# A transformer's third block on one Trainium2 core: router, token rows and routing in one stage, the table of rows by products of one-hot matrices, and LayerNorm in one stage

## What is computed

```python
hB = jax.nn.silu(layer_norm(hB, conv_ln_g, conv_ln_b))
yB = hB * jax.nn.silu(zB)
...
return layer_norm(r, ln_g, ln_b)
```

```python
logits = (h @ router_w + router_b).astype(jnp.float32)
top_v, top_i = lax.top_k(logits, TOP_K)
...
row_tok = jnp.full((n_blocks * MOE_BLOCK,), T, jnp.int32).at[dest].set(tok_sorted)
h_pad = jnp.concatenate([h, jnp.zeros((1, D), h.dtype)], axis=0)
xs = h_pad[row_tok].reshape(n_blocks, MOE_BLOCK, D)
```

## Time and profile before

| | |
|---|---|
| runs, us | 3936.74, 3937.1 (median), 3944.75 |
| profiled execution, us | 3943.41 |
| its span, us | 3941.2 |
| TensorE busy | 3407.6 us, 86% of the span |
| VectorE busy | 2309.9 us, 59% |
| ScalarE busy | 1537.9 us, 39% |
| GpSimd busy | 140.9 us, 4% |
| mean granted TensorE clock | 0.917 of full |

### The profile page before, as it was taken

How to read it: one execution, slowest core, us unless ns; L and a number is a source line. 1 busy time by engine, 2 the same in 40 slices (tenths; PEclk the granted TensorE clock), 3 DMA queues, 4 the chain that set the end, 5 groups by cost and what they waited for, 6 DMA issues and landing times. The chain is left out here.

```text
span 3941.2 us, 47465 instructions
## 1 busy us (share of the span) xinstructions
PE 3407.6 (86%) x16455; PEld 2632.6 (67%) x16456; DVE 2309.9 (59%) x2974; ACT 1537.9 (39%) x1920; POOL 140.9 (4%) x131
## 2 busy tenths in 40 slices
PE   7778898999968687899987977839999999999996
PEld 6546786874446467788764845637777777777774
DVE  4255765337322146455544384438888888888885
ACT  1154332010023341110113143217777777777772
POOL 0000000000000100000000000020000000000001
PEclk9879999999979888699997989959999999999997
DMA  5321222222111100022345201139999999999996
GB/s 168 92 70 33 85 96 84 97 86 86 65 32 48 33 17 1 17 93 98 105 152 205 96 1 41 47 140 411 363 352 351 355 361 351 358 356 359 355 348 227
DMA packets 189602, 653.68 MB, mean 166 GB/s; under 512 B 15081, under 2 KB 101193, under 8 KB 133042
## 3 DMA queue, kind: packets, MB, share of 16 engines
q1 hardware_dynamic: 171650, 605.44, 42.7%
q0 software_dynamic: 7568, 25.70, 1.7%
q10 hardware_dynamic: 10272, 21.02, 1.4%
HBM read 611.02 MB, written 36.77 MB: 164 GB/s over the span
## 5 line engine op out<-in xcount | busy, mean ns | idle before, releaser
L450 DVE TENSOR_TENSOR experts_rest<-experts_weights,experts_leading 128x2048 fp32r<-128x2048 f32 x384 | 875.1, 2286 | 100.0 <-ACT experts_leading L3122 100.0
L3122 ACT CAST experts_leading<-experts_weights 128x2048 fp32r<-128x2048 f32 x384 | 717.5, 1904 | 48.7 <-ACT experts_y L3114 24.3
L456 PE MATMUL psum<-experts_leading,experts_xT_leading 128*128 128x512 f32 x1024 | 411.7, 402 | 50.2 <-DVE experts_rest L450 50.2
L458 PE MATMUL psum<-experts_leading,experts_xT_rest 128*128 128x512 f32 x1024 | 410.7, 401 | 0.0
L457 PE MATMUL psum<-experts_rest,experts_xT_leading 128*128 128x512 f32 x1024 | 410.2, 401 | 0.0
L456 PEld LDWEIGHTS psum<-experts_leading,experts_xT_leading 128*128 128x128 f32 x1024 | 194.9, 190 | 109.1 <-DVE experts_rest L450 64.2
L457 PEld LDWEIGHTS psum<-experts_rest,experts_xT_leading 128*128 128x128 f32 x1024 | 195.9, 191 | 47.2
L458 PEld LDWEIGHTS psum<-experts_leading,experts_xT_rest 128*128 128x128 f32 x1024 | 195.8, 191 | 45.1
L456 PE MATMUL psum<-experts_leading,experts_hidden_leading 128*128 128x512 f32 x512 | 209.3, 409 | 0.0
L458 PE MATMUL psum<-experts_leading,experts_hidden_rest 128*128 128x512 f32 x512 | 203.0, 396 | 0.0
L457 PE MATMUL psum<-experts_rest,experts_hidden_leading 128*128 128x512 f32 x512 | 202.3, 395 | 0.0
(11 more groups left out here) (738 smaller groups left out, 6899.8 us busy)
## 6 DMA issues: line engine op xcount, KB each, us to landing
experts_weights<-in_w_up SPq DMA_DIRECT2D x256, 1024.0 KB, 6.8
experts_weights<-in_w_down SPq DMA_DIRECT2D x128, 1024.0 KB, 6.0
ada_unit<-in_w_ada SPq DMA_DIRECT2D x12, 2048.0 KB, 16.8
expert_rows<-experts_y ACTq DMA_DIRECT2D x66, 256.0 KB, 7.1
merge_first<-in_w_merge SPq DMA_DIRECT2D x16, 768.0 KB, 4.3
merge_weights<-in_w_merge SPq DMA_DIRECT2D x16, 768.0 KB
ff_up_first<-in_w_up SPq DMA_DIRECT2D x11, 1024.0 KB, 4.8
ff_up_weights<-in_w_up SPq DMA_DIRECT2D x11, 1024.0 KB
```

The source lines that it names most:

```text
L450: return dve.tensor_tensor(out, src, leading.bitcast(F32), ALU.subtract)
L456: pe.matmul(out, lh, rh, start=start, stop=False)
L458: return pe.matmul(out, ll, rh, start=False, stop=stop)
L3122: act.copy(leading[h % LEADING], place(ring, h)).then_inc(masked, 1)
```

## The change

- `feature_norm` can center: the chunks are summed in four stripes, ScalarE keeps the negative mean, TensorE spreads it to four banks, VectorE adds it to each chunk, and ScalarE alone squares. It can also apply another function than Identity with the shift, and multiply at the end. `feature_center`, and for branch B `activate` and `multiply`, are no longer called.
- The router's weights and bias and the experts' first bias are loaded in `moe_norm`.
- `route` takes in the tokens' rows and the router. The logits are formed with the weights as stationary operand, in four stripes that are then added by four small products. The rows' copies out of PSUM go to ScalarE.
- The 16 scatters, the fill, the load and the turn are gone. The table of rows is the sum of 16 products: (tokens' lane one-hot, 128 by 128) times (block one-hot weighted by token minus 512, 128 by 48).
- The first block's gather is issued at the end of `route`.

Diff, cut:

```diff
+def feature_norm(k, name, groups, scale, eps, shift=None, memory=(), then=None, center=False, func=ACT.Identity, times=None):
...
+                if center:
+                    act.wait_ge(added, 1)
+                    act.activation(mean[:, :], k.bank(2, P), ACT.Copy, scale=-1.0 / (len(flat) * P)).then_inc(averaged, 1)
...
+                    if center:
+                        act.wait_ge(centered, i + 1)
+                    if center or i % 2 == 0:
...
                         act.activation(sq[:, i % 4, 0:width[g]], s, ACT.Square).then_inc(squared[0], 1)
...
-                    act.activation(o, o, ACT.Identity, bias=shift[n]).then_inc(shifted, 1)
+                    act.activation(o, o, func, bias=shift[n]).then_inc(shifted, 1)
...
+                if center:
+                    for i, (_, _, s) in enumerate(flat):
+                        for j in range(STRIPES):
+                            last = pe.matmul(k.psum[j * STRIPE:(j + 1) * STRIPE, 2 * BANK:2 * BANK + P], k.c("ones")[:, 0:STRIPE],
+                                             s[:, j * P:(j + 1) * P], start=(i == 0), stop=(i == len(flat) - 1))
+                    last.then_inc(added, 1)
+                    pe.wait_ge(picked, 1)
+                    pe.wait_ge(averaged, 1)
+                    for j in range(STRIPES):
+                        rows = slice(j * STRIPE, (j + 1) * STRIPE)
+                        last = pe.matmul(k.bank(4 + j, P), first_rows[rows, :], mean[rows, :], start=True, stop=True)
+                    last.then_inc(placed, 1)
...
+                if center:
+                    dve.wait_ge(placed, 1)
+                    for _, _, s in flat:
+                        dve.tensor_tensor(striped(s), striped(s), striped(k.psum[:, 4 * BANK:8 * BANK])[:, :, 0:P], ALU.add
+                                          ).then_inc(centered, 1)
...
+                for n, (o, other) in enumerate(times or ()):
+                    dve.wait_ge(shifted, n + 1)
+                    dve.tensor_tensor(o, o, other, ALU.mult).then_inc(gated, 1)
...
-def feature_center(k, name, srcs):
...
-    feature_center(k, "ln2_center", chunks)
     feature_norm(k, "ln2", [(chunks, [k.x[:, n, :] for n in range(KD)], [k.p("ln_g", n) for n in range(KD)])],
-                 1.0 / D, "eps_2", shift=[k.p("ln_b", n) for n in range(KD)], then=ctx_load)
+                 1.0 / D, "eps_2", shift=[k.p("ln_b", n) for n in range(KD)], then=ctx_load, center=True)
...
-        feature_center(k, "conv_center", chunks)
         w_qc = first_unit(k, "proj2c", Section(d["w2_q_c"], 2, KD, None, None, None, chunks=2))
         feature_norm(k, "conv_ln", [(chunks, chunks, [k.p("conv_ln_g", n) for n in range(4)])], 1.0 / 512,
-                     "eps_2", then=w_qc.load)
-        activate(k, "conv_silu", ACT.Silu, [(acc[:, n, :], acc[:, n, :], k.p("conv_ln_b", n)) for n in range(4)])
-        multiply(k, "conv_gate", [(y[:, 4 + n, :], y[:, 4 + n, :], acc[:, n, :]) for n in range(4)])
+                     "eps_2", then=w_qc.load, shift=[k.p("conv_ln_b", n) for n in range(4)], center=True, func=ACT.Silu,
+                     times=[(y[:, 4 + n, :], acc[:, n, :]) for n in range(4)])
...
+    def load(self, k):
+        def then(sp, sem):
+            sp.dma_start(self.w[:, :], k.dram["router_w"][0, :, :]).then_inc(self.landed[0], 16)
+            sp.dma_start(self.bias[:, :], k.dram["router_b"][0:1, :].broadcast_to([P, EXPERTS])).then_inc(self.landed[0], 16)
+            sp.dma_start(self.b1[:, :], k.dram["b1_3"]).then_inc(self.landed[1], 16)
+        return then
...
+            @block.sync
...
+                sp.dma_start(residual, k.x[:, :, :].rearrange("p k t -> p (k t)")).then_inc(stored, 16)
+                sp.wait_ge(cleared, 1)
+                sp.dma_start(rows[T:T + 1, :], zero[:, :]).then_inc(rows_stored, 16)
+                for t in range(TT):
+                    sp.wait_ge(copied, 2 * t + 2)
+                    sp.dma_start(rows[t * P:(t + 1) * P, :], by_token[:, t, :]).then_inc(rows_stored, 16)
+                sp.wait_ge(rows_stored, 16 * (TT + 1))
+                sp.wait_ge(stored, 16 * 3)
+
+            @block.gpsimd
...
+                pool.memset(zero[:, :], 0.0).then_inc(cleared, 1)
+                pool.wait_ge(kept, 1)
+                pool.tensor_copy(index[:, 0:1], row_of[:, 0:1]).then_inc(indexed, 1)
+                pool.wait_ge(rows_stored, 16 * (TT + 1))
+                pool.wait_ge(indexed, 1)
+                pool.indirect_dma_start(out=x_rows[:, 0, :], out_offset=None, in_=rows,
+                                        in_offset=bass.IndirectOffsetOnAxis(ap=index[:, 0:1], axis=0)).then_inc(first_gathered, 16)
...
+                act.wait_ge(counted, 1)
+                act.copy(iota[:, :], k.bank(2, P)).then_inc(iota_kept, 1)
+                act.wait_ge(parted, 1)
+                act.copy(part_sums[:, :], k.bank(0)).then_inc(part_copied, 1)
+                act.wait_ge(b1_raised, 1)
+                act.activation(b1_leading[:, :], inputs.b1[:, :], ACT.Copy).then_inc(b1_masked, 1)
...
+                for n in range(2 * TT):
+                    act.wait_ge(turned, n + 1)
+                    act.copy(by_token[:, n // 2, (n % 2) * BANK:(n % 2 + 1) * BANK], k.bank(4 + n % 4)).then_inc(copied, 1)
...
+                act.wait_ge(blocked, 1)
+                for t in range(TT):
+                    mine = in_block[:, t, :, :].rearrange("p k b -> p (k b)")
+                    act.activation(mine, mine, ACT.Copy, scale=token[:, t:t + 1]).then_inc(weighted, 1)
...
+                pe.matmul(k.bank(2, P), k.c("ones"), k.c("before")[:, 0:P], start=True, stop=True).then_inc(counted, 1)
+                pe.wait_ge(inputs.landed[0], 32)
+                for kk in range(KD):
+                    j = kk % STRIPES
+                    last = pe.matmul(k.psum[j * STRIPE:(j + 1) * STRIPE, 0:T], inputs.w[:, kk * E:(kk + 1) * E], k.h[:, kk, :],
+                                     start=(kk < STRIPES), stop=(kk >= STRIPES))
+                last.then_inc(parted, 1)
+
...
+                turn(0)
+                pe.wait_ge(part_copied, 1)
+                for t in range(TT):
+                    last = pe.matmul(k.psum[:, BANK + t * E:BANK + (t + 1) * E], part_sums[:, t * P:(t + 1) * P], k.c("striped"),
+                                     start=True, stop=True)
+                last.then_inc(summed, 1)
+                for n in range(1, 2 * TT):
+                    turn(n)
...
+                pe.wait_ge(choice, TT)
...
+                last.then_inc(ranked, 1)
...
+                for t in range(TT):
+                    pe.wait_ge(weighted, t + 1)
+                    pe.wait_ge(laned, t + 1)
+                    for n in range(K):
+                        last = pe.matmul(k.psum[:, 6 * BANK:6 * BANK + B], in_lane[:, t, n, :], in_block[:, t, n, :],
+                                         start=(t == 0 and n == 0), stop=(t == TT - 1 and n == K - 1))
+                last.then_inc(placed, 1)
+                pe.wait_ge(passed_, 1)
...
+                pe.wait_ge(spreaded, TT)
+                for t in range(TT):
+                    last = pe.transpose(k.psum[0:E, 7 * BANK + t * P:7 * BANK + (t + 1) * P], spread[:, t, :], k.c("ident"))
+                last.then_inc(gated, 1)
...
+                dve.wait_ge(summed, 1)
+                v.do(dve.tensor_tensor(logits[:, :, :], k.psum[:, BANK:BANK + TT * E].rearrange("p (t e) -> p t e", e=E),
+                                       inputs.bias[:, :].unsqueeze(1).broadcast_to([P, TT, E]), ALU.add))
...
-                v.then(dve.tensor_copy(toks[:, :], k.c("lanes_on")))
-                v.then(dve.memset(fill[:, :], T))
...
+                v.do(dve.tensor_scalar(ratio[:, :, :], dest_f[:, :, :], 1.0 / P, None, ALU.mult))
+                dve.wait_ge(iota_kept, 1)
+                v.do(dve.tensor_tensor(edges[:, :, :, :].rearrange("p t k b -> p (t k) b"),
+                                       iota[:, 0:B + 1].unsqueeze(1).broadcast_to([P, TT * K, B + 1]),
+                                       ratio[:, :, :].rearrange("p t k -> p (t k)").unsqueeze(2).broadcast_to([P, TT * K, B + 1]),
+                                       ALU.is_le))
+                dve.tensor_tensor(in_block[:, :, :, :], edges[:, :, :, 0:B], edges[:, :, :, 1:B + 1], ALU.subtract).then_inc(blocked, 1)
+                v.do(dve.tensor_reduce(block_of[:, :, :], edges[:, :, :, 1:B], AX_X, ALU.add))
+                v.do(dve.scalar_tensor_tensor(lane_of[:, :, :], block_of[:, :, :], float(-P), dest_f[:, :, :], ALU.mult, ALU.add))
+                for t in range(TT):
+                    dve.tensor_tensor(in_lane[:, t, :, :], iota[:, :].unsqueeze(1).broadcast_to([P, K, P]),
+                                      lane_of[:, t, :].unsqueeze(2).broadcast_to([P, K, P]), ALU.is_equal).then_inc(laned, 1)
+                v.then(dve.tensor_scalar(dest[:, :, :], dest_f[:, :, :], float(P), None, ALU.add))
...
```

(28 more changed lines are left out.)

221 lines of the change are left out of this document (95 added, 126 removed).

## The result

The changed kernel takes 3878.8 us (median of 4 runs, 3877.9 to 3882.7) against 3939.6 us for the kernel before beside it (3936.7 to 3944.8): ratio 0.984, 95% interval [0.982, 0.985], or 60.8 us less. The forecast was 3882.5, 54.6 us less than the 3937.1 from which it was worked out.

What follows compares the result with a forecast made beforehand. TensorE paces the experts; the touched stretches are single-step chains with engines mostly waiting. Gains of 9.1, 7.6 and 37.9 us sum to 54.6, taken from the median 3937.1 to forecast 3882.5 us, range 3868 to 3897.

Steps and rivals of the forecast that it cites:

- Branch B's LayerNorm: Four stages become one, 24.25 us before and 15.2 after: 9.1 us gained.
- The last one: The last LayerNorm, 26.54 us before and 18.4 after: 8.1 us gained, 7.6 after a late weight unit.
- Unit 11 of the modulation weights late by 0.5 us: Modulation after the last LayerNorm: its last weight unit lands late by 0 to 1.3 us, taken as 0.5.
- Router to ranks: Merged routing stage, from its start through router, logits and row turning to the ranks: 12.0 us.
- Ranks to destinations: Routing, from ranks to destinations: unchanged at 11.8 us, ending 23.8 us into the stage.
- the clock rises in the long stage: Rival for routing: denser work nearly halves ranks and 16 products, 3 to 7 us less, total 3877; chance 0.13.
- One-hots: Routing's row table: edges, blocks and sum on VectorE 2.9 us, then 16 products at 7.3 us.
- From the table to the experts' begin: Routing's end: block map, gates, turning, copy and boundary take 6.1 us, so the experts begin at 41.5.
- The head: Experts' start to first product: 14.0 us instead of 19.0, bound by the weights' landing; 5.0 us gained.
- The gather: First gather, issued at about 36.6, lands 7.5 us later, 2.6 us into the experts.
- The experts' blocks: Experts after their first product: no gain counted, since nothing there changes but their start.
- The rival that ends slower: Experts: their phase against the clock changes, TensorE falls to half level more often, total 3960; chance 0.02.

Runs made afterwards that it cites:

- e4_products_twice: The changed kernel with the sixteen products of the one-hots repeated into an unused part of PSUM: 3887.9 us.
- e3_gather_behind: The changed kernel with the first gather issued at the start of the experts' stage instead of at the end of routing: 3887.3 us.
- e9_early_head: The changed kernel with the experts' weight loads started before GpSimd's clears and SiLU's table touched first: 3875.8 us.
- e7_pause: The changed kernel with thirteen copies on ScalarE between routing and experts, a pause of about 8 us: 3888.3 us.
- e1_layernorms: The kernel before with only the two LayerNorms changed, old routing: 3932.5 us against 3943.6 for the kernel before beside it.
- e12_all_64: The changed kernel with every buffer at a multiple of 64 bytes, weights loaded before GpSimd's clears and SiLU's table touched first: 3889.2 us.
- e6_pad: The changed kernel with one unused tile of 32 bytes per partition ahead of the experts' buffers: 3859.3 us.
- e13_before_all_64: The kernel before with every buffer at a multiple of 64 bytes: 3930.0 us against 3948.0 for the kernel before beside it.
- e5_scatters: The changed kernel with the row table made by sixteen scatters and a read, as before, instead of one-hots and products: 3891.4 us.

## Why the prediction was right

The stages that the sum counts gained 58.5 us for 54.6. The LayerNorms gave 1.0 more than their terms, routing 3.5 more, of which 3.0 are the clock, and the head 0.7 less (terms are rounded). The experts gained 8.9 that no term held, and 3.4 were lost where nothing was changed: 64.0 between the spans. So the chains were right and the result's nearness to the forecast is in part luck.

- **Branch B's LayerNorm**: 9.2 measured for 9.1. Two errors cancel: the table load is hidden (1.28 less), and the last product ends 1.65 us behind the last SiLU instead of 0.6, since VectorE's four products of 2.49 us queue behind its four scalings (1147.61) and do not lie between them. **The last one**: 8.5 for 8.1; the mean's link took about 1.0 for 1.2, the rest as worked out.
- **Unit 11 of the modulation weights late by 0.5 us**: did not happen. Modulation takes 38.07 us, as before 38.1, though its loads ran 12 us earlier behind the same queue: the queue delivered 413 GB/s in the LayerNorm, more than the 391 that the term took.
- **Router to ranks**: 11.2 for 12.0. **Ranks to destinations**: 8.8 for 11.8. This is the term that was most mis-sized. "Unchanged" was wrong: the rival "the clock rises in the long stage" came true by half, for the ranks and counts (2.0 and 0.9 us less) and not for the sixteen products. The argument against it, the router's unbroken products at 0.50, did not carry over to a stage that begins with striped products and transposes. How much comes of it is the execution's luck: in five of eleven this term is 10.7 to 10.9 us. (Two slips of the working stay under its rounding: the router's terms add up to 6.5 us and not 6.6, and 0.29 and 0.68 us give 1.02 ns an element more, not 1.05.)
- **One-hots**: edges, blocks and sum took 2.86 us for 2.9; the products 7.03 for 7.3, whole on the path (`e4_products_twice`). The trace's 0.214 us a pass held (6.8 us for 32 of them). The Trainium skill (TensorE: Matmul & The Clock Gate, LDWEIGHTS) would have it at 0.107 and, as an estimate by that, the sum at 41.3; by it the products would have ended some 3.4 us sooner than they did. The twenty passes of the ranks took 2.42 us at the full level, 0.12 each, so the page's figure is near what this trace shows at that level and half of what it shows at the other. From the table to the experts' begin: 6.6 us for 6.1; the gates end the stage there, so the gather's wait on GpSimd costs nothing.
- **The head**: 14.6 for 14.0, 4.3 gained for 5.0; the table load was left behind the wrong cover. The gather, taken to land 2.6 us into the experts, had landed before they began; its 7.5 us were those of a gather beside the weights' loads. That the gather had been the bound, and the weights were next, is what `e3_gather_behind` and `e9_early_head` show from both sides.
- **The experts' blocks**: counted at zero, they gained 8.0 us. "Nothing in the experts changes but their start" was wrong: their buffers moved. It is neither the phase (`e7_pause`) nor the LayerNorms (`e1_layernorms`). The rival that ends slower had the right place, TensorE's pace in the experts, and the wrong cause and sign; `e12_all_64` shows how a change as good as this one can lose 10 of its us there, and `e6_pad` gains 15.
- Measured without the 31 blocks the change is worth 56.0 us between the two profiled executions (64.0 less 8.0) and 52.8 between the medians (60.8 less 8.0). With every buffer at a multiple of 64, `e13_before_all_64` against `e12_all_64`, it is 40.8, plus 16.0 for the blocks, less the 4 us of the head's edits: 53. The sum of 54.6 was right for the change within 2 us; the 60.8 of the result also has its buffers' luck in it.

## What to carry to other kernels

Before a change of less than one per cent is judged, look at a stage that it does not touch: if that has moved, set it apart, and try the same kernel with a few unused bytes ahead of its buffers. A chain of single steps can be costed from its rows to within a microsecond where its clock stays, but each shortened chain uncovers what it had covered: here the weights' landing and a table load stood behind the gather. A landing is only as long as in the row it was read from when the same transfers run beside it. Where a merged stage changes what TensorE does ahead of a step, that step's clock is not its old one: cost it at both levels.

## What the runs showed of the hardware that was not expected

- One product of 128x512 in the experts starts 227.7 (`e6_pad`), 231.4 (the changed kernel) or 232.9 ns (before) after the last, on average over the blocks without a fall, for the same instructions at granted clock 1.00, with buffers shifted by 32 bytes to 8 KB. VectorE's and ScalarE's busy times hardly move with it (995 to 998 us, 871 to 873).
- The falls of the clock to its half level inside dense work last 3.4 us each. In the kernel before they stand 153.6 us apart, or four blocks; in the changed kernel 228.7, or six, once 303.7. The quicker the products, the fewer, by and large (3 to 8 in 31 blocks). Blocks without a fall differ too, so the falls alone do not make the difference.
- A stage on GpSimd that ends with an indirect DMA's issue stayed open behind it: 4.8 us to GpSimd's next instruction in `e5_scatters`, where nothing else was left to do.
- Landings of one and the same load differ between executions by 2 us: the first bias 3.8 (before) and 6.1 us (`e1_layernorms`). The first gather of 128 rows lands in 4.2 to 4.3 us when it is issued before the weights' loads, and in 7.5 (before) to 8.9 us (`e3_gather_behind`) beside them.
